# A hybrid decoder layer on one core: the seventh token block split in the mixer steps, three engines' orders changed at the change of blocks

## The reference

```python
h = rms_norm(x, norm_w)
proj = einsum('btd,de->bte', h, w_in) + b_in        # 8720 columns
attn = sliding_window_sink_attention(a_q, a_k, a_v, attn_sinks)      # first mixer
branch_a = einsum('bte,ed->btd', attn * silu(a_z), w_branch_attn)
h_tilde = mlstm_chunkwise(mq, mk, m_v, m_i, m_f)                     # second mixer
h_m = sigmoid(m_o) * head_rms_norm(h_tilde, mlstm_norm_w) * silu(m_z)
branch_m = einsum('bte,ed->btd', h_m, w_branch_mlstm)
merged = sigmoid(g_attn) * branch_a + sigmoid(g_mlstm) * branch_m
y = rms_norm(x + einsum('btd,de->bte', merged, w_out), final_norm_w)
```

## Time and profile before

| what | value |
|---|---|
| time, median of 3 | 1075.77 us (1075.28 to 1076.61) |
| profiled execution | 1076.66 us, its span 1075.0 us |
| TensorE busy | 1055.8 us, 98% |
| VectorE, GpSimd, ScalarE busy | 72%, 64%, 50% |
| granted TensorE clock, mean | 0.997 |
| DMA | 129.68 MB, 121 GB/s over the span |

### The profile page before, as it was taken

How to read it: one execution, slowest core, us unless ns; L and a number is a source line. 1 busy time by engine, 2 the same in 40 slices (tenths; PEclk the granted TensorE clock), 3 DMA queues, 4 the chain that set the end, 5 groups by cost and what they waited for, 6 DMA issues and landing times.

```text
span 1075.0 us, 18676 instructions
## 1 busy us (share of the span) xinstructions
PE 1055.8 (98%) x6343; PEld 854.6 (80%) x6343; DVE 774.4 (72%) x1184; ACT 539.3 (50%) x1283; POOL 687.2 (64%) x469
## 2 busy tenths in 40 slices
PE   7999999999999999999999999999998899999997
PEld 6887887877877888878888888788776788888886
DVE  5964785776866967766776686669588657766897
ACT  7544755746647643555345444545566335113443
POOL 3577555556555568668965796569678985545441
PEclk9999999999999999999999999999999999999999
DMA  6225132132151232214321333142338338676424
GB/s 221 71 93 89 41 118 80 41 121 76 45 159 41 80 118 79 89 41 146 120 80 50 123 105 114 39 127 88 99 110 309 129 119 310 218 273 256 175 83 151
DMA packets 120973, 129.68 MB, mean 121 GB/s; under 512 B 7804, under 2 KB 97208, under 8 KB 119368
## 3 DMA queue, kind: packets, MB, share of 16 engines
q1 hardware_dynamic: 106520, 83.37, 25.3%
q10 hardware_dynamic: 14384, 45.42, 12.3%
HBM read 95.12 MB, written 33.65 MB: 120 GB/s over the span
## 4 chain that ended last, share of the span: by engine, by line
PE 89%; POOL 3%; DVE 2%; DMA 2%; ACT 2%; DVEq 1%; issue 1%; POOLq 1%; ACTq 0%; SPq 0%
PE ps L1092 67%; PE ps L1396 5%; PE ps L999 4%; PE ps L1210 3%; PE ps L1191 2%; POOL ring_lo L825 2%; PE ps L1265 2%; PE ps L1337 1%; PE ps L1319 1%; DMA u_raw<-u_sums_scratch 1%; PE ps L1334 1%; DVE u_m L2680 1%; PE ps L1331 1%; PE ps L1285 1%; PE ps L1352 1%; PE ps L1324 1%
## 5 line engine op out<-in xcount | busy, mean ns | idle before, releaser
L825 POOL TENSOR_TENSOR ring_lo<-w,ring_hi 128x512 fp32r<-128x512 f32 x144 | 210.6, 1484 | 85.8 <-ACT ring_hi L1528 85.7
L825 POOL TENSOR_TENSOR ring_lo<-t,ring_hi 128x512 fp32r<-128x512 f32 x108 | 153.8, 1429 | 143.8 <-ACT ring_hi L1528 143.8
L1092 PE MATMUL ps<-s_hi,ring_hi 128*128 128x512 f32 x576 | 228.7, 397 | 1.1 <-issue 1.1
L1092 PE MATMUL ps<-s_lo,ring_hi 128*128 128x512 f32 x576 | 225.1, 391 | 0.0
L1092 PE MATMUL ps<-s_hi,ring_lo 128*128 128x512 f32 x576 | 225.0, 391 | 0.0
L1092 PE MATMUL ps<-h_hi,ring_hi 128*128 128x512 f32 x432 | 171.5, 397 | 6.2 <-POOL ring_lo L825 3.3
L1092 PE MATMUL ps<-h_lo,ring_hi 128*128 128x512 f32 x432 | 169.6, 393 | 0.0
L1092 PE MATMUL ps<-h_hi,ring_lo 128*128 128x512 f32 x432 | 169.1, 391 | 0.0
L1528 ACT ACTIVATE ring_hi<-w 128x512 fp32r<-128x512 f32 x144 | 86.7, 623 | 108.9 <-PE ps L1092 98.7
L1092 PEld LDWEIGHTS ps<-s_hi,ring_hi 128*128 128x128 f32 x576 | 108.2, 188 | 25.0 <-issue 4.0
L1092 PEld LDWEIGHTS ps<-s_hi,ring_lo 128*128 128x128 f32 x576 | 108.2, 188 | 22.5
(11 more groups left out here) (315 smaller groups left out, 2072.7 us busy)
## 6 DMA issues: line engine op xcount, KB each, us to landing
w<-in_w_in SPq DMA_DIRECT2D x128, 256.0 KB, 2.9
xs<-in_x SPq DMA_DIRECT2D x8, 512.0 KB, 8.2
ga_scratch<-ev ACTq DMA_DIRECT2D x4, 1024.0 KB, 4.2
u_scratch<-silu_z ACTq DMA_DIRECT2D x8, 512.0 KB, 3.2
c_rows<-c_scratch ACTq DMA_DIRECT2D x8, 512.0 KB, 6.8
ev<-u_scratch SPq DMA_DIRECT2D x8, 512.0 KB, 4.7
u_sums_scratch<-ev ACTq DMA_DIRECT2D x4, 1024.0 KB, 4.3
gm_scratch<-ev ACTq DMA_DIRECT2D x4, 1024.0 KB, 5.1
```

The source lines that it names most:

```text
L825: return nc.gpsimd.tensor_tensor(flat(lo[:]), flat(raw_or_sum[:]), flat(hi[:]).bitcast(F32), ALU.subtract)
L1092: mm = nc.tensor.matmul(ps[:, bank, columns], w[:, k, :], h[:, k, columns], start=(m == 0), stop=(m == PRODUCT - 1))
```

## The change

Block 6 is split ahead: in each mixer step ScalarE rounds its quarter sum into a new tile `us_hi`, VectorE puts the low part in place into `ev`, and ScalarE stores both; at the change of blocks SyncE loads the two parts, and TensorE waits for the load. GpSimd's sums for the last step are made one pair earlier. In the branch's pairs GpSimd's order is t1, low w11, t2, low t2, w12, low w21, low w12, t4, low t4, low t1, low w22, and SyncE loads w21 after w12 in all but the first. ScalarE splits blocks 1 to 5 later in its list and makes the root of the heads' norms in pair 32; VectorE's list is changed likewise.

```diff
+                sp.wait_ge(w7_ready, n)
+                sp.dma_start(w12[:], wba_cols[:, 0:KH, second]).then_inc(w12_in, 16)
+                if a:
+                    sp.wait_ge(sum_made, 4 * n)
+                    lower_left()
...
+                if n == 6:
+                    sp.dma_start(s4[0][:].bitcast(F32), scr_uh.rearrange("k p n -> p k n")).then_inc(u_in[n], 16)
+                    into = s4[1][:].bitcast(F32)
+                sp.dma_start(into, src.rearrange("k p n -> p k n")).then_inc(u_in[n], 16)
...
+            def first_of_branch_pair(i):
+                pool.drain()
+                pool.wait_ge(w11_in, 16 * i + 16)
+                pool.wait_ge(w12_in, 16 * i + 16)
+                add(t1[:], w12[:], w11[:], ALU.subtract).then_inc(sum_made, 1)
+                pool.wait_ge(w1_hi, i + 1)
+                low(w11, ring0).then_inc(w1_ready, 1)
+                pool.drain()
+                pool.wait_ge(w22_in, 16 * i + 16)
+                add(t2[:], w22[:], t1[:], ALU.subtract).then_inc(sum_made, 1)
+                pool.wait_ge(w6_hi, i + 1)
+                low(t2, ring1).then_inc(w6_ready, 1)
+                add(w12[:], w22[:], w12[:], ALU.subtract).then_inc(sum_made, 1)
+
+            def rest_of_branch_pair(i):
+                pool.wait_ge(w2_hi, i + 1)
+                low(w21, ring2).then_inc(w2_ready, 1)
+                pool.wait_ge(w7_hi, i + 1)
+                low(w12, ring3).then_inc(w7_ready, 1)
+                add(t4[:], w21[:], t2[:], ALU.subtract).then_inc(sum_made, 1)
+                pool.wait_ge(w4_hi, i + 1)
+                low(t4, ring0).then_inc(w4_ready, 1)
+                pool.wait_ge(w5_hi, i + 1)
+                low(t1, ring1).then_inc(w5_ready, 1)
+                pool.wait_ge(w3_hi, i + 1)
+                low(w22, ring4).then_inc(w3_ready, 1)
...
-            weights_of_pair(WPAIRS - 2, hook=last_branch_sums)
+            weights_of_pair(WPAIRS - 3, hook=last_branch_sums)
+            weights_of_pair(WPAIRS - 2)
...
-                        pe.wait_ge(blocks, q + 1)
-                        if q == 6:
-                            ORDER[q](i0, 0, PRODUCT - TERMS, None)
-                            pe.wait_ge(blocks, q + 2)
-                            a = PRODUCT - TERMS
+                        if q < 6:
+                            pe.wait_ge(blocks, q + 1)
+                        else:
+                            pe.wait_ge(u_in[q], 32)
...
-                us_chunk = 7 if last else 3
+                us_chunk = 4 if last else 3
+                us_store = 6 if last else 4
...
-                    if last and q == 1:
-                        block_high(0)
-                        block_high(1)
-                    if last and q >= 4:
-                        block_high(q - 2)
+                    if last:
+                        for n in {1: (0,), 4: (1,), 5: (2, 3), 6: (4,)}.get(q, ()):
+                            block_high(n)
...
                     if c == us_chunk:
-                        act.wait_ge(us_made, p + 1)
+                        act.wait_ge(us_made, 2 * p + 1)
+                        act.sem_inc(passed, 1)
+                        A(us_hi[:], ev[:, 1, token_half(0)], ACT.Copy).then_inc(s_hi, 1)
+                    if c == us_store:
+                        act.drain()
+                        act.wait_ge(us_made, 2 * p + 2)
+                        act.dma_start(scr_uh[ds(p, 1)].rearrange("a p n -> p (a n)"), us_hi[:].bitcast(F32)).then_inc(us_out, 16)
...
-                    if a == 0 and q in (0, 1):
-                        block_high(5 + q)
+                    if a == 0 and q == 0:
+                        block_high(5)
                     if a == 0 and q == 2:
                         store_gm(PAIRS - 1)
+                        head_roots(PAIRS - 1)
...
-                    if last and q in (2, 3):
-                        block_low(q - 2)
-                    if last and q == 5:
-                        block_low(2)
-                    if last and q == 6:
-                        block_low(3)
-                        block_low(4)
+                    if last:
+                        for n in {2: (0,), 5: (1,), 6: (2, 3)}.get(q, ()):
+                            block_low(n)
...
+                def branch_sum_low():
+
+                    dve.wait_ge(s_hi, 4 + p + 1)
+                    dve.sem_inc(passed, 1)
+                    part = ev[:, 1, token_half(0)]
+                    V.tensor_tensor(part.bitcast(F32R), part, us_hi[:].bitcast(F32), ALU.subtract).then_inc(us_made, 1)
...
+                    if c == (5 if last else 3):
+                        branch_sum_low()
...
                     if a == 0:
                         if q == 1:
+                            block_low(4)
                             block_low(5)
-                        if q == 2:
-                            block_low(6)
```

More of the change, by code:

```diff
@@ L606, in _, with pair_weights @@
             sp.dma_start(before_rc[:, :], scr_before.rearrange("h (c a) -> (h c) a", a=1)).then_inc(g_moved, 16)
-            def pair_weights(i, n1, n2, first=False, src=w_cols, between=None):
+            def pair_weights(i, n1, n2, first=False):
                 n = i if isinstance(i, int) else sp.snap(i)
@@ L615, in pair_weights @@
                 sp.sem_inc(passed, 1)
-                sp.dma_start(w11[:], src[:, 0:KH, ds(c1, P)]).then_inc(w11_in, 16)
+                sp.dma_start(w11[:], w_cols[:, 0:KH, ds(c1, P)]).then_inc(w11_in, 16)
                 sp.wait_ge(w2_ready, n)
                 sp.sem_inc(passed, 1)
-                sp.dma_start(w21[:], src[:, KH:KT, ds(c1, P)]).then_inc(w21_in, 16)
-                if between is not None:
-                    between()
+                sp.dma_start(w21[:], w_cols[:, KH:KT, ds(c1, P)]).then_inc(w21_in, 16)
                 sp.wait_ge(w7_ready, n)
                 sp.sem_inc(passed, 1)
-                sp.dma_start(w12[:], src[:, 0:KH, ds(c2, P)]).then_inc(w12_in, 16)
+                sp.dma_start(w12[:], w_cols[:, 0:KH, ds(c2, P)]).then_inc(w12_in, 16)
                 sp.wait_ge(w3_ready, n)
                 sp.sem_inc(passed, 1)
-                sp.dma_start(w22[:], src[:, KH:KT, ds(c2, P)]).then_inc(w22_in, 16)
+                sp.dma_start(w22[:], w_cols[:, KH:KT, ds(c2, P)]).then_inc(w22_in, 16)
             def attention_weights(g):
@@ L666, in _, with branch_weights, lower_left @@
             ended(sp, PAIRS, mlstm_weights)
-            def branch_weights(a, between=None):
-                n1, n2 = ROWS_OF[a]
-                pair_weights(WPAIRS + a, n1 * P, n2 * P, src=wba_cols, between=between)
+            def branch_weights(a):
+                n, (n1, n2) = WPAIRS + a, ROWS_OF[a]
+                first, second = slice(n1 * P, (n1 + 1) * P), slice(n2 * P, (n2 + 1) * P)
+                def lower_left():
+                    sp.dma_start(w21[:], wba_cols[:, KH:KT, first]).then_inc(w21_in, 16)
+                sp.wait_ge(w1_ready, n)
+                sp.dma_start(w11[:], wba_cols[:, 0:KH, first]).then_inc(w11_in, 16)
+                if a == 0:
+                    sp.wait_ge(w2_ready, n)
+                    lower_left()
+                    sp.wait_ge(p1_done, WPAIRS)
+                    tokens_block(0)
+                sp.wait_ge(w7_ready, n)
+                sp.dma_start(w12[:], wba_cols[:, 0:KH, second]).then_inc(w12_in, 16)
+                if a:
+                    sp.wait_ge(sum_made, 4 * n)
+                    lower_left()
+                sp.wait_ge(w3_ready, n)
+                sp.dma_start(w22[:], wba_cols[:, KH:KT, second]).then_inc(w22_in, 16)
             def tokens_block(n):
@@ L895, in _ @@
             weights_of_pair(0)
-            with pool.Fori(1, WPAIRS - 2) as i:
+            with pool.Fori(1, WPAIRS - 3) as i:
                 weights_of_pair(i)
-            weights_of_pair(WPAIRS - 2, hook=last_branch_sums)
+            weights_of_pair(WPAIRS - 3, hook=last_branch_sums)
+            weights_of_pair(WPAIRS - 2)
             weights_of_pair(WPAIRS - 1)
-            weights_of_pair(WPAIRS, new_tokens=True)
-            for i in range(WPAIRS + 1, SPAIRS):
-                weights_of_pair(i)
+            for i in range(WPAIRS, SPAIRS):
+                first_of_branch_pair(i)
+                rest_of_branch_pair(i)
             for j in range(2):
@@ L1931, in mlstm_step @@
                 retire(chunks_end(count) + 20)
-                act.wait_ge(m_var, p + 1)
-                A(rstd[:], rstd[:], ACT.Sqrt).then_inc(m_root, 1)
+                if not last:
+                    head_roots(p)
                 retire(count * PAIR)
```

44 lines of the change are left out of this document (20 added, 24 removed).

## The result

The changed kernel takes 1083.91 us (median of 6 runs, 1082.70 to 1086.20) against 1075.45 for the kernel before (6 runs, 1075.03 to 1076.61): ratio 1.0078, 95% interval 1.0068 to 1.0089. It is slower by 8.5 us. The two profiled executions stand 8.6 apart (1076.66 and 1085.26). The forecast was 1080.4 with a range up to 1083.5: the direction and the place were right, the size was not.

The account below looks back on a forecast made before the run. TensorE bounds it, losing 9.4 us at the change to the branch, with VectorE and GpSimd as one queue. Loads 5.4 late less a 1.2 lead, plus 0.4 for the clock: +4.6 us, 1080.4; range 1078 to 1083.5, with rivals 1074.5 to 1083.5.

Parts of the forecast that it names:

- the forecast's mechanism: End of pair 35: late low w22 delays the second branch's weight and token loads, so TensorE enters that branch 4.2 us later.
- Mixer steps at no cost: Mixer steps: the added ScalarE copy, VectorE subtraction and store, and the earlier GpSimd sums, cost 0 us (0 to 2).
- the split gives next to nothing: Change of blocks: the last block's split frees 2.15 us of the shared VectorE/GpSimd queue, none of TensorE directly.
- First gap goes: Before pair 32's first product: TensorE's gap of 1.63 us disappears, as ScalarE's high part now comes first.
- second 3.4 with a slow clock: Before pair 32's third product: a gap of 3.4 us in place of 2.89, with 1.5 us lost to the low clock.
- a new one of 2.55 ahead of pair 33's second product: Pair 33: low t2 queues behind VectorE's normalisation, so TensorE waits 2.55 us; 0 if GpSimd comes first, 4 if clock falls.
- The lead of 1.2 us: Up to pair 34: TensorE some 1.2 us ahead of the kernel before; bounds 9.4 ahead or 0.5 behind.
- the third gap, forecast at 0.75: Before pair 32's sixth product: low t1 comes later, leaving a TensorE gap of 0.75 us in place of 1.12.
- Low w22 of pair 35 5.4 us late: End of pair 35: low w22, now last, ends at 894.9, 5.4 us late on an unmoved TensorE (bounds 4.4 and 6.0).
- 0.4 us for a chance that the clock falls at the second branch: Second branch's start: the clock falls in about a quarter of cases, 1.5 us, counted as 0.4 in the sum.
- VectorE's first low part in front of the addition for the bank is over in time: Second branch's tokens: the wait for the addition freeing TensorE's bank, to 904.5, is over before the last load's.
- Nothing is given back: Behind the second branch's start: later work moves along with the loads; it left 0.19 us of slack, so the lateness stays.

Follow-up runs that it names:

- w22 early in 33 to 35: The kernel after, with GpSimd making low w22 right behind the sum t4, ahead of low t4 and low t1, in pairs 33 to 35; 1077.89 us.
- w22 early in 35: The kernel after, with GpSimd making low w22 right behind the sum t4, ahead of low t4 and low t1, in pair 35 alone; 1079.55 us.
- gate products late: The kernel after, with VectorE's two gate products of pair 35 moved behind its fourth product's additions; 1082.06 us.
- normalisation held back: The kernel after, with VectorE's normalisation of the heads waiting until GpSimd has made low t2 of pair 33; 1081.35 us.
- before, w22 last in 35: The kernel before, with low w22 of pair 35 moved from third to last of its run, behind low t1; 1080.30 us.
- w22 early in 33, 34: The kernel after, with low w22 right behind the sum t4 in pairs 33 and 34 only, still last in pair 35; 1083.34 us.
- ScalarE, VectorE undone: The kernel after, with ScalarE's and VectorE's orders of the kernel before and GpSimd's new order kept; 1085.18 us.
- GpSimd's order undone: The kernel after, with GpSimd's order of the kernel before in all four branch pairs, ScalarE's and VectorE's new orders kept; 1075.95 us.
- the kernel without the wait ahead of block 1: The kernel after with GpSimd's old order, but low w11 of pair 33 ahead of sum t2, and the heads' normalisation waiting for low t2; 1071.87 us.

## Why the prediction was wrong in size and right in kind

The profiled executions side by side (us; lateness against the kernel before in brackets) carry the main point. They are single executions, up to 3 us from their kernels' medians:

| kernel | branch weight issued | last token high part begins | profiled execution |
|---|---|---|---|
| before | 889.58 | 906.19 | 1076.66 |
| w22 early in 33 to 35 | 891.31 (1.7) | 906.67 (0.5) | 1077.87 (1.2) |
| w22 early in 35 | 892.82 (3.2) | 908.16 (2.0) | 1079.55 (2.9) |
| gate products late | 895.00 (5.4) | 911.72 (5.5) | 1082.30 (5.6) |
| normalisation held back | 896.76 (7.2) | 913.80 (7.6) | 1084.39 (7.7) |
| before, w22 last in 35 | 896.79 (7.2) | 912.38 (6.2) | 1083.00 (6.3) |
| w22 early in 33, 34 | 897.26 (7.7) | 912.64 (6.5) | 1083.63 (7.0) |
| ScalarE, VectorE undone | 898.02 (8.4) | 914.36 (8.2) | 1085.18 (8.5) |
| after | 898.80 (9.2) | 914.68 (8.5) | 1085.26 (8.6) |

The end is late by what the last high part is late, to within 1 us, and that by what the loads are late, to within 1.3: the forecast's mechanism holds in every kernel whose loads go out late. In the five others of the experiments the loads go out by 890 and the end follows TensorE's own position instead, to within 0.9 us: with GpSimd's order undone, for one, the last matmul of pair 35 begins 1.4 us earlier than before, the last high part 2.7 and the execution is 1.2 shorter.

- *Mixer steps at no cost; the split gives next to nothing*: nothing contradicts it. With all orders as before the early split is +0.7 us, interval -0.2 to +1.7 (expected -0.5, at most +0.5).
- *First gap goes; second 3.4 with a slow clock; a new one of 2.55 ahead of pair 33's second product, with the normalisation begun just before low t2*: right to 0.3 us. They are the 3.44 and 2.30 at the top; the normalisation began at 842.47, low t2 at 842.96, and the run that held it back took the gap to 0.88.
- *The lead of 1.2 us*: gone, 0.13 at the end of pair 35. At the first product of pair 33 TensorE leads by 3.79 us (840.76 against 844.55), where the forecast's terms give 3.75. That was luck: the low clock behind the second gap cost 2.8 us and not 1.5 (the third product took 5.26 us, 4.29 before), but the third gap, forecast at 0.75, didn't come, and pair 32 began 0.5 earlier than forecast (815.36). The new gap then took 2.3 us of the lead and the low clock behind it 1.4 (0.78 and 0.50), which the forecast had as a bound ("4 if the clock falls too") and not in the sum. The lead lost is 1.1 us.
- *Low w22 of pair 35 5.4 us late*: the step that failed. It was 9.2 late with TensorE at its old place. The 3.8 us are three terms. (a) A loop that I did not see, 1.5 us: the load of w22 waits for low w22 of the pair ahead, now the last of its pair; it went out at 877.90 (870.56 before), landed beside two gate rows from ScalarE's queue by 883.9, six microseconds on, and the sum t2 waited 2.27. The run with w22 early in pairs 33 and 34 took 1.5 off the issue, with TensorE 0.5 later in that trace; so (a) may be up to 2.1 and (c) as little as 0.8. (b) Two gate products cost two stays in the port queue (4.50 against 2.53 us), the forecast counted one of 1.1: 0.9. (c) The rest, 1.4: the forecast bounded the start of low t1 by TensorE's product (891.3), but with the sums t2, w12 and t4 behind low w11 the limit is GpSimd itself, ten operations of 1.25 us with two waits of 0.74 for ScalarE's high parts. Without the loop low t4 still starts at 891.43, and low t1 1.25 behind it. This term is read from the traces; no run takes it away by itself.
- *0.4 us for a chance that the clock falls at the second branch*: it fell in the kernel after (0.50 from 910 to 914) and cost nothing: even at half speed TensorE's weight loads wait for the last high parts, 0.49 us at 914.83 and 0.44 at 915.77. In three of the late kernels (w22 early in 35 and in 33 to 35; before with w22 last) it didn't fall.
- *VectorE's first low part in front of the addition for the bank is over in time*: right for the end, though TensorE's wait is put down to it: the addition at 908.84 came behind that low part (907.09), when the first two high parts were done by 908.0 (906.01 and 2.00 us for both). It holds up TensorE's start at 909.57, which the loads don't let matter, since the last high part begins 5 us later.
- *Nothing is given back*: right in the main. The issue's 9.2 are 8.5 at the last high part, 0.7 better than one to one; from the issue to the last high part the traces of all kernels took 15.3 to 17.1 us, 16.6 before.

In numbers: forecast 4.6; lead lost +1.1; low w22 +3.8; clock not paid -0.4; loads a little quicker -0.7: 8.4, against 8.6 measured in the profiled executions.

Two of my later expectations missed by much: with GpSimd's order undone the landing of w22 in pair 33 was left out again (expected -5, no difference), and with w22 early in 33 and 34 the terms (b) and (c) were (expected +4.6, measured +8.1). Smaller misses are told with their runs.

The Trainium skill's page "SBUF — State Buffer" (section "Who interferes with whom") has the port locked for whole instructions. The trace agrees: in the kernel after, an operation of 1.3 us on GpSimd beside a block subtraction takes 3.34 us, and each gate product that falls beside the weights' low parts adds 1.0.

## What to carry to other kernels

When an operation is moved to the end of a list because its reader needs it late, look at everything its completion releases: here low w22 also freed the buffer for the next w22 and the space and queue for five loads of the next stage, and those, not TensorE's product, were its first deadline. A queue that is walked has to be walked with its releases (who may load into what), over more than one turn of the loop. And an engine at the limit makes "by need" orders costly: sums that can be made early, while the engine waits, should be.

## What the runs showed of the hardware

- Behind gaps of 2.30 us (846), 3.37 (842, GpSimd undone), 3.44 (824) and 5.55 (909.6) the granted clock fell to 1.2 GHz; behind gaps of 0.88, 1.42 and 1.53 it stayed at 2.4 GHz. The length of the gap alone doesn't decide it: in the kernel with the gate products late a gap of 3.44 us at the same place left the clock at full, as the two rows below show. So four gaps of 0.65, 0.33, 0.32 and 1.53 us (2.83 in all, GpSimd undone) cost less than the one of 2.30 with 1.7 us of slow clock behind it (granted 0.78, 0.50 and 0.87 over three stretches of 2 us).

```profile
824.43 0.47 PE L1134 MATMUL ps<-h_hi,ring_hi 128*128 128x512 f32 x1 [3.44 <-issue]
```

```profile
826.00:828.00 2.00, 2.00 (x11) 1.65 (x10) 1.73 (x1) 0.00 (x0) 2.00 (x1) 1.00 0.67 188
```

- In the kernel without the wait ahead of block 1 five runs took 1071.5 to 1072.1 us, and its profiled one 1074.5. That trace suggests why such a kernel can jump; the others have none to compare. Beside the trace of the kernel that differs from it by the normalisation's wait alone, w11 and w12 landed 1.0 us later (GpSimd's first sum at 807.94 in place of 806.90), low t2 came to the port 0.5 us behind VectorE's block 1 (815.02 and 814.48) and not 0.4 ahead of it (813.99 and 814.40), and TensorE's gap at the third product was 3.60 us in place of 0.90.
- The w22 load of pair 35, 256 KB beside two gate rows on ScalarE's queue, took 6.0 us in the kernel after (877.90 to 883.91) and 3.9 in the one with the gate products late (878.14 to 882.05). The median of the sixteen loads of this kind in the kernel after is 3.4. Between these two traces its landing alone moved GpSimd by 1.9 us.
